# First layer's projections in the order u, v, gate 0, q, k; phasors moved to GpSimd; a loop of six half projections; another order of ScalarE's steps

## What is computed

```
xn = rms_norm(x, norm_mix[layer]);  proj = xn @ w_in[layer]        # 1024 x 4096
q, k, v, u = four blocks of 512 columns;  gates = sigmoid(last 2048 columns)
a = diff_attention(rotary(q), rotary(k), v, lam)                   # 4 heads, two softmaxes each
a = rms_norm(a, attn_subln[layer]) * (1 - lam_init)
s = gelu(s5_bidirectional(u, ...))                                 # 32 groups, 64 complex states, 2 directions
s = s * sigmoid(s @ w_glu[layer])
merged = gates[0] * (a @ w_branch[layer, 0]) + gates[1] * (s @ w_branch[layer, 1])
x = x + merged @ w_out[layer]
x = x + (swiglu(hn) in layer 0, top-2-of-8 expert swiglu in layer 1)   # hn = rms_norm(x, norm_ffn)
```

## Time and profile before

| what | value |
|---|---|
| median of 3 runs | 1546.03 us (1545.55 to 1546.53) |
| profiled execution, its own time | 1545.13 us |
| its span, first to last instruction | 1543.3 us, so 1.8 us lie around it |
| TensorE / VectorE / ScalarE / GpSimd busy | 92% / 74% / 58% / 20% |
| mean granted TensorE clock | 0.972 |
| stages of the span (from the timeline) | layer 0: first part to 119, loop to 209, rest of the mixer to 298; feed-forward to 471; layer 1: first part to 550, loop to 639, rest to 722; experts to 1543 |

### The profile page before, as it was taken

One profiled execution on the slowest core, in us unless ns is written; L12 is line 12 of the kernel. 1 busy time (PEld: TensorE's weight loads), 2 busy tenths in 40 slices (PEclk: granted clock), 3 DMA queues, 4 the chain that ended last, 5 costly groups with the idle time before them and its releaser, 6 DMA issues.

```text
span 1543.3 us, 24088 instructions
## 1 busy us (share of the span) xinstructions
PE 1423.8 (92%) x8701; PEld 1165.2 (76%) x8701; DVE 1146.9 (74%) x1125; ACT 894.3 (58%) x986; POOL 309.6 (20%) x354
## 2 busy tenths in 40 slices
PE   5688969999998989698999999999999999999995
PEld 3476748788887777487788888888878888888884
DVE  6966637655446556376888889888898899888985
ACT  4234544544335355444776777777677677676774
POOL 3747741998000067100000000000000000000000
PEclk9899979999999999898999999999999999999998
DMA  9332234555554423194999999999999999999970
GB/s 267 103 103 86 95 95 162 180 169 191 193 183 145 157 71 109 54 337 156 321 369 340 350 344 341 359 331 353 365 317 360 336 350 363 323 359 321 359 268 27
DMA packets 273808, 374.64 MB, mean 243 GB/s; under 512 B 17616, under 2 KB 220752, under 8 KB 273616
## 3 DMA queue, kind: packets, MB, share of 16 engines
q1 hardware_dynamic: 270176, 367.51, 70.8%
q0 software_dynamic: 1280, 3.15, 1.1%
q10 hardware_dynamic: 2288, 3.11, 0.6%
HBM read 371.63 MB, written 1.05 MB: 241 GB/s over the span
## 4 chain that ended last, share of the span: by engine, by line
PE 77%; DVE 8%; ACT 5%; issue 5%; DMA 1%; SPq 1%; POOL 1%; DVEq 0%; ACTq 0%; POOLq 0%
PE bank L549 75%; ACT hi L1016 3%; DVE lo L1362 3%; PE bank L946 1%; SPq L424 1%; PE bank L567 1%; DVE at_lo L1778 1%; DMA raw<-in_w_out_dram 1%; DMA areg<-in_norm_mix_dram 1%; DVE at_lo L1748 1%; DVE at_lo L1376 0%; PE bank L860 0%; PE bank L704 0%; POOL raw L1893 0%; ACT raw L1104 0%
## 5 line engine op out<-in xcount | busy, mean ns | idle before, releaser
L1362 DVE TENSOR_TENSOR lo<-raw,hi 128x2048 fp32r<-128x2048 f32 x347 | 805.2, 2325 | 191.4 <-ACT hi L1016 182.2
L1016 ACT ACTIVATE hi<-raw 128x2048 fp32r<-128x2048 f32 x347 | 662.9, 1914 | 115.0 <-PE bank L549 112.9
L549 PE MATMUL bank<-hi,at_hi 128*128 128x512 f32 x1280 | 518.3, 405 | 35.4 <-DVE areg L1414 13.7
L549 PE MATMUL bank<-hi,at_lo 128*128 128x512 f32 x1280 | 503.6, 393 | 0.0
L549 PE MATMUL bank<-lo,at_hi 128*128 128x512 f32 x1280 | 503.4, 393 | 0.0
L549 PEld LDWEIGHTS bank<-hi,at_hi 128*128 128x128 f32 x1280 | 242.9, 190 | 89.7 <-issue 17.3
L549 PEld LDWEIGHTS bank<-hi,at_lo 128*128 128x128 f32 x1280 | 242.8, 190 | 52.2
L549 PEld LDWEIGHTS bank<-lo,at_hi 128*128 128x128 f32 x1280 | 243.7, 190 | 46.1
L549 PE MATMUL bank<-hi,ht_hi 128*128 128x512 f32 x440 | 172.2, 391 | 4.4 <-DVE ht_lo L1679 3.5
L549 PE MATMUL bank<-hi,ht_lo 128*128 128x512 f32 x440 | 171.3, 389 | 0.0
L549 PE MATMUL bank<-lo,ht_hi 128*128 128x512 f32 x440 | 171.3, 389 | 0.0
(11 more groups left out here) (265 smaller groups left out, 1096.5 us busy)
## 6 DMA issues: line engine op xcount, KB each, us to landing
raw<-in_moe_w_dram SPq DMA_DIRECT2D x528, 512.0 KB, 5.5
raw<-in_ffn_w_dram SPq DMA_DIRECT2D x66, 512.0 KB, 4.2
raw<-in_w_in_dram SPq DMA_DIRECT2D x64, 512.0 KB, 4.6
raw<-in_w_branch_dram SPq DMA_DIRECT2D x16, 512.0 KB, 4.1
raw<-in_w_out_dram SPq DMA_DIRECT2D x16, 512.0 KB, 4.9
raw<-in_w_glu_dram SPq DMA_DIRECT2D x4, 512.0 KB, 4.2
xres<-in_x_dram SPq DMA_DIRECT2D x2, 512.0 KB, 6.1
areg<-in_norm_mix_dram ACTq DMA_DIRECT2D x2, 512.0 KB, 6.4
```

Of the source, the lines that this page charges most:

```text
L549: return pe.matmul(o, a, b, start=start, stop=stop)
L1016: act.activation(hi[:, slot, :], src, ACT.Copy).then_inc(hi_ready, 1)
L1362: tt(lo[:, slot, :], src, hi[:, slot, :].bitcast(f32), SUB).then_inc(lo_ready, 1)
```

## The change

- Layer 0 loads and projects u, v, gate block 0, q, k ahead of the loop, and gate blocks 1 to 3 in it (`LOOP_PROJ`: a tile in steps 0, 1, 3, 4, 6, 7, none in steps 2 and 5). Layer 1 projects u, v, q, k and then has eight tiles in the loop as before.
- Gate block 0 now needs its place in `gates` early, so the powers of B keep 12 of 16 pairs there and 4 elsewhere (`bpre_end`); a `product` that touches them is done in two parts, 12 instructions in place of 6.
- `phasors` of layer 0 goes from VectorE to GpSimd, after `c_chain` in both layers. `inner` stands ahead of the transposes of k, and ScalarE copies its result after both rotaries.
- In the loop TensorE does `scores(s,0)` ahead of `s5_in(s+1)`. ScalarE does the copy of the turned weights (`weights_back`) and `scale_second` first, then the gate's Tanh, then the rest of `head_back`. In step 7 it does Gelu after `scale_second`.
- After the loop `channels` stands ahead of `head_out(7)`, its copies ahead of Sqrt, and the attention's transposes after proj t+16.

The order, and a product in two parts:

```diff
-W_IN_ORDER = [3, 0, 1, 2, 4, 5, 6, 7]
+W_IN_ORDER = (("u", "v", "g0", "q", "k", "g1", "g2", "g3"), ("u", "v", "q", "k", "g0", "g1", "g2", "g3"))
+LOOP_PROJ = ((0, 1, 3, 4, 6, 7), (0, 1, 2, 3, 4, 5, 6, 7))
...
+            for q0, q1, _ in dst:
+                for r in range(2):
+                    tt(t1[:, r, q0:q1], source(r, q0, q1), num(re, q0, q1), MUL)
+                for r in range(2):
+                    last = tt(t2[:, r, q0:q1], source(1 - r, q0, q1), num(im, q0, q1), MUL)
+            own.step(last)
+            for q0, q1, aps in dst:
+                tt(aps[0], t1[:, 0, q0:q1], t2[:, 0, q0:q1], ADD if conj else SUB)
+                last = tt(aps[1], t1[:, 1, q0:q1], t2[:, 1, q0:q1], SUB if conj else ADD)
+            own.step(last)
```

TensorE, first part, then loop, then behind it:

```diff
-                proj(t + 4, l, 2, 0, True, False)
-                proj(t + 5, l, 2, 4, False, True)
+                for i in range(2, 8 - len(LOOP_PROJ[l]) // 2):
+                    proj(t + 2 * i, l, i, 0, True, False)
+                    proj(t + 2 * i + 1, l, i, 4, False, True)
                 pe.wait_ge(rot_ready, 4 * l + 2)
                 for th in range(TH):
                     transposes((l, "q", th), heads_of(qk[:, 0, :, :], th))
-                proj(t + 6, l, 3, 0, True, False)
-                proj(t + 7, l, 3, 4, False, True)
+                inner(l)
                 pe.wait_ge(rot_ready, 4 * l + 4)
                 for th in range(TH):
                     transposes((l, "k", th), heads_of(qk[:, 1, :, :], th))
-                inner(l)
...
+                    scores(l, s, 0)
                     if s < 7:
                         s5_in(l, s + 1)
-                    scores(l, s, 0)
                     scores(l, s, 1)
...
-                    proj(t + 8 + s, l, 4 + s // 2, 4 * (s % 2), s % 2 == 0, s % 2 == 1)
+                    if s in LOOP_PROJ[l]:
+                        tile, i, half = loop_proj(l, s)
+                        proj(tile, l, i, 4 * half, half == 0, half == 1)
...
                 weights_t(l, 7)
+                channels(l)
                 head_out(l, 7)
-                channels(l)
...
-                proj(t + 16, l, 8, 4, True, True, attention_t)
-                pe.wait_ge(at_lo_ready, at_count(l, "a", 1))
+                proj(t + 16, l, 8, 4, True, True)
+                attention_t()
```

ScalarE, first part, then loop, then behind it:

```diff
+                from_pj(l, 1, t + 3, lambda th: vreg[:, th, :], ACT.Copy, inverse)
...
+                split_static(t + 8)
+                if l == 0:
+                    gate_block(l, "g0", t + 5)
+                for i in range(t + 9, loop_tile(l) + 2):
+                    split_static(i)
...
-                    split_static(t + 10 + s)
+                    if s in LOOP_PROJ[l]:
+                        split_static(loop_proj(l, s)[0] + 2)
                     probs_of(l, s)
...
+                    if s > 0:
+                        weights_back(l, s - 1)
+                    scale_second(l, s)
+                    if s == 7:
+                        act.wait_ge(y_done, DUOS * (l + 1))
+                        for half in range(2):
+                            act.activation(s4[:, 512 * half:512 * half + 512], PY[half][:, :], ACT.Gelu).then_inc(gelu_ready, 1)
+                    if s in LOOP_PROJ[l] and loop_proj(l, s)[2] == 1:
+                        tile, i, half = loop_proj(l, s)
+                        gate_block(l, W_IN_ORDER[l][i], tile)
                     if s > 0:
                         head_back(l, s - 1)
-                    scale_second(l, s)
+                weights_back(l, 7)
+                for th in range(TH):
+                    act.wait_ge(chan_full, 2 * l + th + 1)
+                    act.activation(at_hi[:, 4:8, th * P:(th + 1) * P], PV[th][:, :].rearrange("p (k s) -> p k s", k=4),
+                                   ACT.Copy).then_inc(at_hi_ready, 1)
                 head_back(l, 7)
```

VectorE and GpSimd, first part:

```diff
-                rotary(l, 1, t + 3, qk[:, 0, :, :])
...
-                rotary(l, 2, t + 5, qk[:, 1, :, :])
-                if l == 0:
-                    phasors(dve, own, 0, (area(3072, 512), area(3584, 512)), php_last)
-                    dve.memset(dve_mark, 0.0).then_inc(tabs_ready, 1)
                 inner_diagonal(l)
-                split_static(t + 8)
-                split_static(t + 9)
+                for i in range(t + 6, loop_tile(l)):
+                    split_static(i)
+                rotary(l, "q", qk[:, 0, :, :])
+                split_static(loop_tile(l))
+                split_static(loop_tile(l) + 1)
+                rotary(l, "k", qk[:, 1, :, :])
...
                 c_chain(l)
+                phasors(pool, own, l, (area(14592, 512), area(15104, 512)), php_last)
                 if l == 0:
                     pool.wait_ge(b_part, 1)
```

More of the change, by code:

```diff
@@ L361, in product, with num, source @@
         def product(tt, own, dst, src, j0, re, im, temps, conj):
[L363 to L371 removed]
+            def num(i, q0, q1):
+                n = par[:, i, j0 + 2 * q0:j0 + 2 * q1].rearrange("p (q d) -> p q d", d=2)
+                return n.unsqueeze(3).broadcast_to([P, q1 - q0, 2, GC])
+            def source(r, q0, q1):
+                return next(aps[r][:, q0 - a:q1 - a] for a, b, aps in src if a <= q0 and q1 <= b)
+            t1, t2 = temps
+            for q0, q1, _ in dst:
[8 more added lines that the diff above has]
+            own.step(last)
         def phasors(eng, own, l, temps, squares):
@@ L467, in mixer @@
                 t = T_MIX[l]
-                for n in W_IN_ORDER:
+                for n in (W_IN_COLUMN[name] for name in W_IN_ORDER[l]):
                     for kh in range(2):
@@ L1128, in scan_tables, with gate_block @@
                 last.then_inc(wtab_ready, 1)
+            def gate_block(l, name, tile):
+                g, n = divmod(int(name[1]), 2)
+                from_pj(l, place_of(l, name), tile, lambda th: gates[:, th, g, n * 512:(n + 1) * 512], ACT.Tanh,
+                        lambda th: col(RH + th))
             def mixer(l):
@@ L1201, in mixer @@
                                    ACT.Copy).then_inc(at_hi_ready, 1)
+                head_back(l, 7)
+                act.wait_ge(avar_ready, l + 1)
+                act.activation(col(AR, 8), col(AV, 8), ACT.Sqrt).then_inc(aroot_ready, 1)
                 for th in range(TH):
@@ L1427, in s5_scan @@
                 dve.wait_ge(pv_full, n + 1)
+                if m == 0:
+                    for i in range(2):
+                        dve.memset(decay[i][:, :, 0:1], 0.0)
                 dve.wait_ge(wtab_ready, n + 1)
@@ L1444, in inner_diagonal @@
                 wait_read(dve, (l, "ct", 3))
-                for i in range(2):
-                    dve.memset(decay[i][:, :, 0:1], 0.0)
                 for g in range(2):
@@ L1542, in mixer @@
                     weights(l, s)
+                for h in range(TH):
+                    half = slice(h * P, (h + 1) * P)
+                    dve.wait_ge(at_hi_ready, at_count(l, "sa", h))
+                    tt(at_lo[:, 4:8, half], PV[h][:, :].rearrange("p (k s) -> p k s", k=4),
+                       at_hi[:, 4:8, half].bitcast(f32), SUB).then_inc(at_lo_ready, 1)
                 wait_read(dve, (l, "o", 6))
@@ L1887, in turn_forward @@
                 pool.wait_ge(zs_ready, n + 1)
+                if m == 0:
+                    for edge in xst:
+                        pool.memset(edge[:, :, :, 0:1], 0.0)
+                        pool.memset(edge[:, :, :, 129:130], 0.0)
                 if n > 0:
@@ L1918, in _ @@
                 else:
-                    product(tt, own, bbar, braw, 32, CO_RE, CO_IM, pt, False)
+                    product(tt, own, whole(bbar), whole(braw), 32, CO_RE, CO_IM, pt, False)
                     for k in range(1, 4):
-                        product(tt, own, b_power(k), b_power(k - 1) if k > 1 else bbar, 32, A_RE, A_IM, pt, False)
+                        product(tt, own, b_power(k), b_power(k - 1) if k > 1 else whole(bbar), 32, A_RE, A_IM, pt, False)
                     mark(b_part)
@@ L1924, in _ @@
                 mark(b_ready)
-                pool.wait_ge(tabs_ready, l + 1)
                 phase_products(l, 0)
-                for xs in xst:
-                    pool.memset(xs[:, :, :, 0:1], 0.0)
-                    own.step(pool.memset(xs[:, :, :, 129:130], 0.0))
                 for m in range(DUOS):
```

91 lines of the change are left out of this document (38 added, 53 removed).

## The result

The kernel after takes 1533.01 us (median of 4, 1532.06 to 1538.68) against 1545.79 for the kernel before (1545.37 to 1546.53): ratio 0.9924, 95% interval 0.99 to 0.9949. That is 12.8 us faster; 8.9 were forecast.

What follows compares the result with a forecast made beforehand. It took VectorE, slowed by GpSimd, to bound the first part, a ScalarE-VectorE cycle the loop, a serial chain through ScalarE the tail. Layer 0's -5.5 and layer 1's -3.4 made -8.9: 1537.1 us, range 1530 to 1543.

Steps and rivals of the forecast that it cites:

- part 3: Behind the loop: the serial chain through ScalarE gets shorter, -9.2 us in layer 0 and -6.6 in layer 1.
- The cycle of ScalarE and VectorE: Loop: scale_second, tables, hi, lo, row maximum, scan, factors take 9.98 us; the new order makes steps 10.56, gate steps 11.76.
- Rival (a): Loop: TensorE alone sets it and the new order helps, a step of 9.46 us, 1524.3 in all; chance 0.24.
- less the 0.46 that half_scores no longer idles: Loop, TensorE's own sum for a step: the new order of the scores saves 0.46 us of idling, giving 9.46.
- Part 1: First part of layer 0, ahead of the loop: 9.3 us longer, with two tiles moved there; layer 1's +0.7.
- rival (c): Ahead of layer 0's loop: GpSimd's phasors and last product hold up the "b" blocks, b_ready 14.3 late, 1551.4 us; chance 0.10.
- Part 2, layer 0: Layer 0's loop without two of its tiles: 47.2 us against 53.86 from lo of step 1, so -6.6.
- rival (b): Layer 0's loop: steps without a tile get no shorter, because of GpSimd or the clock, +9.1, 1546.2 us; chance 0.12.
- 3.3 for 5.45 each: Layer 0: each tile taken out of the loop gives back 3.3 us there, where a tile's matmuls take 5.45.
- Part 2, layer 1: Layer 1's loop under ScalarE's new order: 56.4 us for five steps against 53.86, so +2.5.
- scan 7, GpSimd, s5_out(7): The way from step 6 to the end of projection 7, forecast to stay as it was.
- GpSimd's +1.0: End of layer 0's mixer and after: layer 1's GpSimd products start sooner and make VectorE's normalisation wait, +1.0 us (bounds 0 and 3).

Runs made afterwards that it cites:

- e3: The kernel before with only the new order behind the loop, and Gelu in step 7 after the weights' copy and scale_second: 1523.59 us.
- e1: The changed kernel once more, with no edit: 1533.96 us.
- e6: e3 with ScalarE's new order of the loop alone (weights' copy and scale_second ahead of Tanh and head_back): 1528.94 us.
- e2: The changed kernel with the gate's Tanh and head_back ahead of scale_second again, the weights' copy still first: 1533.57 us.
- e11: e7 with ScalarE making the tables of the scan after next ahead of scale_second: 1520.87 us.
- e5: e3 with TensorE's new order of the loop alone, half of the scores ahead of the next s5_in: 1533.78 us.
- e12: The changed kernel with TensorE's order of the loop as before, ScalarE's new order kept: 1533.52 us.
- e8: The changed kernel with TensorE's and ScalarE's orders of the loop both as in e3: 1529.58 us.
- e7: e3 with the weights' copy ahead of the two Tanh in gate steps, Tanh and head_back still ahead of scale_second: 1518.87 us.
- e10: The changed kernel, six projections in layer 0's loop, with TensorE's order of before and ScalarE's of e7: 1522.79 us.
- e4: The changed kernel with layer 0 in layer 1's order, so all eight projections are in its loop: 1535.49 us.
- e9: e4, eight projections in layer 0's loop, with TensorE's order of before and ScalarE's of e7: 1520.26 us.

## Why the prediction came out as it did

**The time.** Faster by 12.8 where 8.9 was forecast, inside the range; but the sum was made of one loss too small and one gain too small, and that they cancel in part is luck. By e3, part 3 gave 21.4 (15.8 forecast). By e1 against e3, parts 1 and 2 together took back 10.4 (the forecast's terms outside part 3 add up to 6.9). Two small slips of the working change nothing: 295.33-288.3 is 7.0, not 6.9, and 5.45+4.4-0.46 is 9.39, not 9.46.

**What bounds the loop.** The cycle of ScalarE and VectorE is real: e6 and layer 1 of the kernel after show steps of 10.3 to 10.6 and 11.8 to 11.9 for 10.56 and 11.76, and e2 takes the gate steps back to 10.48. Rival (a), TensorE at 9.46 a step, is out for this kernel: between `lo` 1 and `lo` 6 no step with a tile and one behind it was below 9.8, but for e11's first (9.04). The sentence "less the 0.46 that half_scores no longer idles" is the step that failed on TensorE's side. The forecast priced the new order of the scores as a small gain; the four score matmuls of e3 leave only 0.1 to gain, and e5 shows +0.43 a step, because a wait for a bank was uncovered, and a longer stretch at the lower clock. In the whole change, beside ScalarE's new order, it adds only 0.4 (e1 over e12).

**Part 1.** The start of layer 0's loop moved by 8.9 (8.4 to 8.9 in after, e1, e2, e12 against the profile of before; 11.0 to 11.6 where old and new first part ran on one chip, e8 against e5 to e7 and e10 against e11) for 9.3. The times within it were right to 2.5 us for VectorE's products and 5 for GpSimd's phasors, and in no kernel with the new first part did `b_ready` hold anything up: rival (c) is out. What was not in it is TensorE's clock: the second tile of gate block 0 took 8.6 us for 5.5 (71.19 to 79.8), and some of q's matmuls ran at 0.63 too, so the "b" blocks began 4.4 late, at 117.91. Nor was it in the forecast that the way from the blocks to `lo` 0 becomes 4.9 shorter. The two cancel, so that the sum of part 1 fits is in part luck. The Trainium skill, "SBUF — State Buffer", Who interferes with whom, says that a VectorE instruction with two inputs in SBUF contends with a GpSimd instruction that reads SBUF. The rows agree and give the price: 1.3 to 1.5 us an instruction in b1, of 384 or of 128 elements, with the exceptions of one pair of 128 and the last two (1.14 and 0.28). e4 and e9 show that this price lay beside TensorE's work.

**Part 2, layer 0.** This is the mis-sized term: -6.6 forecast, -0.95 in the profile of after and -4.2 in e1. Its numbers came out in two kernels (47.10 in e12, 47.19 in e10). Where they did not, projections ran at the lower clock in part (in after those of steps 1 and 3), and that is rival (b)'s clock, in part; that the lower clock alone makes the difference is not shown, since e10's loop has it too (0.88 in 134 to 188, 4.11 us for 72 matmuls in a tile-less step). That the tile-less steps give back less than the two tiles take ahead of the loop was in the forecast, 3.3 for 5.45 each. e9 and e10 put the net price of the gate block ahead of q at 2.5 by the medians and 4.2 by the profiles, and e8 over e3 at 6.0 and 5.2 with all of the new first part; that it is above zero rests on e8 and on the traces, since the intervals of e9 and e10 overlap.

**Part 2, layer 1.** +2.5 forecast, +2.4 measured; with the low clock at the first step +3.7 (e1).

**Part 3.** Layer 0's tail, `lo` to `lo`, fell by 9.9 in after and 10.1 in e3 for 9.2; layer 1's by 7.8 and 8.5 for 6.6. The forecast let the way "scan 7, GpSimd, s5_out(7)" stay. It is worth some 5 us where `lo` of step 7 does not run beside GpSimd's last instructions (tails of 23.0 to 23.1 in e1, e2 and e10), and such a difference between executions of one kernel, 28.00 in after and 23.02 in e1, was in no term. The GLU tile could start 4.1 behind the projection, not 5.75, and ran at the higher clock. Another 1.5 of e3's gain is layer 1's loop, whose first step took 10.25 for 11.81. The 10 us ahead of it ran at a granted clock of 1.00 in e3 and 0.83 in before, but e6 had 11.71 behind 1.00, so the clock is not shown to be the cause. What sets this clock from one execution to the next stays open. Why e12's median is not below e1's is seen in one profile of each, in step 7; whether it is so in the other executions stays open.

**GpSimd's +1.0 in the feed-forward part.** From tile t+19 of layer 0 to layer 1's loop before took 316.6; after 317.0, e1 315.4, e3 315.8, and the others 315.4 to 317.5. No cost is shown.

## What to carry to other kernels

A reordering that brings a small operation forward has to be priced by the wait that the old order covered: the scores ahead of `s5_in` looked free and cost ten microseconds (e5 over e3). Where two engines pass work round a cycle as long as the bound engine's step, put first what another engine waits for (the weights' copy, 0.38 us) and leave late what nobody waits for (the Tanh), but not between the cycle's own links. Time a bundle of edits part by part: here two of its parts lost half of what the third gained, and the bundle still looked like a success. And look for an instruction of one engine that happens to run beside the last link of another's chain: `lo` of step 7 beside GpSimd's last instructions goes with some 3 us of waiting in nearly every mixer here.
